# One layer of a two-block network on one core: S5 outputs one gate unit earlier, groups of seven, and a later second HGRN operand

## What is computed

```python
h = rms_norm(x, mix_norm[l])
(u_a, q_b, f_b, i_b, og_b, cx_c, v_c, o_c, ig_c, fg_c, gates) = jnp.split(h @ w_in[l], splits, axis=-1)
y_a = s5_mixer(u_a, ...)      # complex diagonal recurrence, 32 groups of 16, 64 states
y_b = hgrn2_mixer(q_b, f_b, i_b, og_b, ...)   # gated linear attention, 6 heads, chunks of 64
y_c = mlstm_mixer(cx_c, v_c, o_c, ig_c, fg_c, ...)
merged = (sigmoid(g_a) * (y_a @ wb[:r_a]) + sigmoid(g_b) * (y_b @ wb[r_a:r_b])
          + sigmoid(g_c) * (y_c @ wb[r_b:]))
x = x + merged @ w_out[l]
```

## Time and profile before

| what | value |
|---|---|
| median of 3 runs | 3008.32 us (3007.78 to 3015.89) |
| the profiled execution's own time | 3018.68 us |
| its span in the profile | 3016.9 us |
| TensorE busy (matmuls) | 2962.8 us, 98% of the span |
| VectorE busy | 2051.3 us, 68% |
| ScalarE busy | 1311.4 us, 43% |
| mean granted TensorE clock | 0.994 |
| DMA | 530.39 MB, 176 GB/s |

### The profile page before, as it was taken

One profiled execution on the slowest core, in us unless ns is written; L12 is line 12 of the kernel. 1 busy time (PEld: TensorE's weight loads), 2 busy tenths in 40 slices (PEclk: granted clock), 3 DMA queues, 4 the chain that ended last, 5 costly groups with the idle time before them and its releaser, 6 DMA issues.

```text
span 3016.9 us, 47095 instructions
## 1 busy us (share of the span) xinstructions
PE 2962.8 (98%) x18616; PEld 2640.7 (88%) x18616; DVE 2051.3 (68%) x2624; ACT 1311.4 (43%) x1418; POOL 70.3 (2%) x72
## 2 busy tenths in 40 slices
PE   8999999889999999999999999999999999999999
PEld 8898898889988888888888888886998888888888
DVE  6674787866778888885557776636667666666444
ACT  5354424334444444444444344425444444444333
POOL 0000000000001000000000000000000000000000
PEclk9999999999999999999999999999999999999999
DMA  6553334445555555555555554531455555555555
GB/s 227 182 188 131 119 112 141 140 134 202 183 193 195 195 193 191 190 184 184 187 188 200 194 182 167 182 136 56 168 181 195 191 190 191 194 194 179 193 194 186
DMA packets 87359, 530.39 MB, mean 176 GB/s; under 512 B 9952, under 2 KB 10336, under 8 KB 41184
## 3 DMA queue, kind: packets, MB, share of 16 engines
q1 hardware_dynamic: 87264, 529.07, 50.4%
HBM read 526.94 MB, written 2.10 MB: 175 GB/s over the span
## 4 chain that ended last, share of the span: by engine, by line
PE 94%; DVE 4%; ACT 1%; issue 0%; DMA 0%; SPq 0%; DVEq 0%; ACTq 0%
PE bank L576 72%; PE late L576 22%; DVE arena L1670 2%; DVE half_low L1670 1%; DVE arena L1667 0%; DVE w_low L1670 0%; ACT w_high L1186 0%; DVE arena L1972 0%; PE late L1127 0%; DMA xT<-in_xT 0%; DMA ring<-in_w_gates 0%; DVE acts_both L1670 0%; DVE arena L2087 0%; DVE arena L2088 0%; DVE arena L2030 0%
## 5 line engine op out<-in xcount | busy, mean ns | idle before, releaser
L1670 DVE TENSOR_TENSOR w_low<-ring,w_high 128x2048 fp32r<-128x2048 f32 (+1 forms) x480 | 1014.4, 2114 | 388.4 <-ACT w_high L1186 384.5
L1186 ACT ACTIVATE w_high<-ring 128x2048 fp32r<-128x2048 f32 (+1 forms) x480 | 849.5, 1771 | 649.4 <-DMA ring<-in_w_down 225.9
L576 PE MATMUL bank<-up_early,w_high 128*128 128x512 f32 x1408 | 487.8, 389 | 0.0
L576 PE MATMUL bank<-up_late,w_high 128*128 128x512 f32 x1408 | 487.4, 389 | 0.0
L576 PE MATMUL late<-acts_both,w_high 128*128 128x512 f32 x1408 | 485.8, 392 | 0.3 <-DVE w_low L1670 0.3
L576 PE MATMUL late<-acts_both,w_low 128*128 128x256 f32 x1408 | 391.7, 278 | 0.0
L576 PE MATMUL bank<-up_early,w_low 128*128 128x256 f32 x1408 | 388.7, 276 | 0.0
L576 PE MATMUL bank<-up_late,w_low 128*128 128x256 f32 x1408 | 388.6, 276 | 0.0
L576 PEld LDWEIGHTS late<-acts_both,w_high 128*128 128x128 f32 x1408 | 264.5, 188 | 58.4 <-DVE w_low L1670 0.6
L576 PEld LDWEIGHTS bank<-up_early,w_high 128*128 128x128 f32 x1408 | 264.3, 188 | 55.2
L576 PEld LDWEIGHTS bank<-up_late,w_high 128*128 128x128 f32 x1408 | 264.3, 188 | 55.1
(11 more groups left out here) (311 smaller groups left out, 5041.0 us busy)
## 6 DMA issues: line engine op xcount, KB each, us to landing
ring<-in_w_up SPq DMA_DIRECT2D x176, 1024.0 KB, 4.7
ring<-in_w_down SPq DMA_DIRECT2D x128, 704.0 KB, 4.0
ring<-in_w_in SPq DMA_DIRECT2D x66, 1024.0 KB, 4.7
ring<-in_w_mix SPq DMA_DIRECT2D x62, 1024.0 KB, 4.8
ring<-in_w_gates SPq DMA_DIRECT2D x96, 512.0 KB, 3.7
ring<-in_w_branch SPq DMA_DIRECT2D x16, 1024.0 KB, 4.8
ring<-in_w_out SPq DMA_DIRECT2D x16, 1024.0 KB, 4.7
ring<-in_w_o SPq DMA_DIRECT2D x16, 1024.0 KB, 4.7
```

The costliest lines, as they stand in the source:

```text
L576: return nc.tensor.matmul(o, lhsT, rhs, start=first, stop=last)
L1186: A(w_high[:, s, 0:cols], ring[:, s, 0:cols], ACT.Copy).then_inc(rounded[s], 1)
L1670: return V.tensor_tensor(o, a, b, op)
```

## The change

It does five things in the first block's mixing part. (1) TensorE issues each S5 output one gate unit earlier (after units 23, 30, 37 and 44; before it was after 24, 31, 38 and 43), and the feeds of tiles 2 and 3 after units 27 and 34 in place of 26 and 33. (2) VectorE's `s5_kept(f - 1)` moves from before the four products from PSUM to behind the two sums, where only a wait for the output stays before the products (they overwrite what that output's matmuls read). Each of the tiles 1 to 3 now has seven lowerings. Before these were six, seven and seven; tile 0 has five in place of four. One lowering stands in the middle of the scans. (3) The output matrix is made in two parts, the second behind the last rotation. (4) In the HGRN levels `meet(2)` and the lowering of gate unit 8 move behind the copies of level 0, and the memset of `HPR` moves to before the mLSTM's normalisation. (5) The first two branch units do their 12 HGRN and mLSTM k-tiles first, without the wait for `s5_gate`, and then their 4 S5 k-tiles. The number of instructions on SyncE, TensorE and ScalarE is the same, and SyncE's order is unchanged.

```diff
-GATES_FED = 44
+GATES_FED = 46
...
@@ TensorE
             for c in range(19, GATES_FED):
                 gate()
-                if c in (21, 26, 33):
-                    s5_feed({21: 1, 26: 2, 33: 3}[c])
-                if c in (24, 31, 38):
-                    s5_output({24: 0, 31: 1, 38: 2}[c])
-            s5_output(3)
+                if c in (21, 27, 34):
+                    s5_feed({21: 1, 27: 2, 34: 3}[c])
+                if c in (23, 30, 37, 44):
+                    s5_output({23: 0, 30: 1, 37: 2, 44: 3}[c])
             for c in range(GATES_FED, GATES):
                 gate()
...
-            def branches(first):
-                def body(s):
-                    for o, lo, hi in ((bank[s][:, 1], 4, 10), (bank[RING + s][:, 0], 10, 16), (bank[s][:, 0], 0, 4)):
-                        if first:
-                            pe.wait_ge(y_lowered, 3 if lo == 0 else 2)
-                            pe.wait_ge(s5_gate, 1)
-                        for k in range(lo, hi):
-                            last = mm3(o, s, k, *y[k], k == lo, k == hi - 1)
-                    return last
-                return body
...
+            def branch_parts(s, first):
+                for o, lo, hi in ((bank[s][:, 1], 4, 10), (bank[RING + s][:, 0], 10, 16)):
+                    if first and lo == 4:
+                        pe.wait_ge(y_lowered, 2)
+                    for k in range(lo, hi):
+                        mm3(o, s, k, *y[k], k == lo, k == hi - 1)
...
+            pair = []
+            for j in range(2):
+                s, _, _, _, free = units.next(split=True)
+                pe.wait_ge(lowered[s], units.lowered[s].value())
+                if not isinstance(free, int) or free > 0:
+                    pe.wait_ge(drained[s], free)
+                branch_parts(s, j == 0)
+                pair.append(s)
+            pe.wait_ge(y_lowered, 3)
+            for s in pair:
+                branch_s5(s).then_inc(consumed[s], 1)
+            for j in range(2):
+                unit_split(branches)
+            rounds_split(3, branches)
...
@@ VectorE, the way into the HGRN levels
             row_factors()
             lower_gate()
+            V.memset(HPR, 1.0)
             dve.wait_ge(norm_spread, casts[0])
...
             dve.wait_ge(norm_done, 2)
 
 
-            lower_gate()
-            link(V.memset(HPR, 1.0))
             dve.wait_ge(hg_x, 1)
-            dve.wait_ge(hmask_landed, 16)
             meet(1)
-            meet(2)
+            dve.wait_ge(hmask_landed, 16)
+
             for lvl in range(9):
                 dve.wait_ge(hg_scored, lvl + 1)
...
-                if 1 <= lvl <= 6:
+                if lvl == 0:
+                    lower_gate()
+                if lvl <= 6:
                     meet(lvl + 2)
                 if lvl < 8:
                     lower_gate()
...
@@ VectorE, S5
-            def s5_output_matrix():
+            def s5_output_matrix(part):
...
-                    s5_kept(f - 1)
+                    dve.wait_ge(s5_out, f)
                 dve.wait_ge(s5_fed, f + 1)
...
                 if f == 0:
-                    s5_output_matrix()
+                    s5_output_matrix(0)
+                else:
+                    s5_kept(f - 1)
                 lower_gate()
                 for n in range(4):
                     m = mag[:, 4 * f + n:4 * f + n + 1].broadcast_to([P, T])
                     V.tensor_tensor_scan(tmp_r[:, n], m, SR[:, n], 0.0, M, ADD)
                     last = V.tensor_tensor_scan(tmp_i[:, n], m, SI[:, n], 0.0, M, ADD)
+                    if n == 1:
+                        lower_gate()
                 link(last)
                 lower_gate()
                 link(tt(SR, turn_c, tmp_r))
                 link(tt(SI, turn_s, tmp_r))
                 link(tt(tmp_r, turn_s, tmp_i))
                 tt(tmp_i, turn_c, tmp_i).then_inc(s5_states, 1)
+                dve.wait_ge(s5_states, f + 1)
+                if f == 0:
+                    s5_output_matrix(1)
                 lower_gate()
-                dve.wait_ge(s5_states, f + 1)
-                if f > 1:
-                    lower_gate()
-            s5_kept(S5_TILES - 1)
             for c in range(GATES_FED, GATES):
                 lower_gate()
+                if c == GATES_FED + 1:
+                    s5_kept(S5_TILES - 1)
```

More of the change, by code:

```diff
@@ L972, in _, with branch_s5, branches @@
                 y += [(y_high[:, 6 * m + k], y_low[:, at + k]) for k in range(6)]
-            def branches(first):
-                def body(s):
-                    for o, lo, hi in ((bank[s][:, 1], 4, 10), (bank[RING + s][:, 0], 10, 16), (bank[s][:, 0], 0, 4)):
-                        if first:
-                            pe.wait_ge(y_lowered, 3 if lo == 0 else 2)
-                            pe.wait_ge(s5_gate, 1)
-                        for k in range(lo, hi):
-                            last = mm3(o, s, k, *y[k], k == lo, k == hi - 1)
-                    return last
-                return body
[L985 to L988, removed]
+            def branch_parts(s, first):
[4 more added lines that the diff above has]
+                        mm3(o, s, k, *y[k], k == lo, k == hi - 1)
+            def branch_s5(s):
+                for k in range(4):
+                    last = mm3(bank[s][:, 0], s, k, *y[k], k == 0, k == 3)
+                return last
+            def branches(s):
+                branch_parts(s, False)
+                return branch_s5(s)
+            pair = []
[12 more added lines that the diff above has]
+            rounds_split(3, branches)
             merged_out(out_both)
@@ L1979, in _ @@
             lower_gate()
[L1981 to L1986, removed]
-            lower_gate()
[L1988 to L1995, removed]
-            lower_gate()
-            link(V.memset(HPR, 1.0))
-            dve.wait_ge(hg_x, 1)
-            dve.wait_ge(hmask_landed, 16)
             def halves(ap, B):
@@ L2018, in meet @@
                     link(tt(pf[:, :, 1], pf[:, :, 1], pf[:, :, 0, B - 1:B].broadcast_to(n)))
+            for h in range(HG):
+                last = (V.tensor_scalar(HF[:, h], HF[:, h], lb[:, 1, h:h + 1], lb[:, 0, h:h + 1], M, ADD))
+            link(last)
+            V.tensor_scalar(HK, HF, -1.0, 1.0, M, ADD).then_inc(hg_x, 1)
+            V.memset(PD, 0.0)
+            row_factors()
+            lower_gate()
+            V.memset(HPR, 1.0)
+            dve.wait_ge(norm_spread, casts[0])
+            for h in range(ML):
+                for k, p0, p1, _ in PIECES[h]:
+                    c = VAT["ml_norm"] + k
+                    last = stt(HH[p0:p1, k], HH[p0:p1, k], vec[p0:p1, c:c + 1], factor(h)[p0:p1])
+            link(last)
+            tt(MT[:, O0:O0 + 6], HH, MT[:, O0:O0 + 6]).then_inc(norm_done, 1)
+            dve.wait_ge(norm_done, 2)
+            dve.wait_ge(hg_x, 1)
             meet(1)
-            meet(2)
+            dve.wait_ge(hmask_landed, 16)
             for lvl in range(9):
@@ L2048, in _ @@
             lower_gate()
-            def s5_output_matrix():
+            def s5_output_matrix(part):
                 re, im = (x.rearrange("p (n o) -> p n o", o=1).broadcast_to([P, S5_STATES, S5_ROWS]) for x in (cr, ci))
[L2052 to L2058, removed]
+                if part == 0:
+                    dve.wait_ge(s5_c_landed, 16)
+                    link(tt(c_new, c_re, re))
+                    link(tt(c_tmp, c_im, im))
+                    link(tt(c_new, c_new, c_tmp, SUB))
+                else:
+                    link(tt(c_tmp, c_re, im))
+                    link(tt(c_im, c_im, re))
+                    tt(c_im, c_im, c_tmp, ADD).then_inc(s5_c_made, 1)
             def s5_kept(f):
```

1 line of the change is left out of this document (removed).

## The result

The changed kernel takes 2984.13 us (median of 4 runs, 2982.29 to 2985.54), the kernel before 3012.11 us (median of 4, 3007.78 to 3017.72). The ratio is 0.9906, 95% interval 0.9884 to 0.9927: 28 us, 0.9%, less. Forecast were 27.2 us less and 2981.1 us. The profiled execution took 2985.54 us, 33.1 us less than that of before, which is more than the medians differ. Counted up to the 37th matmul of the branch units, close to where the change ends, the two traces differ by 26.8 us (696.03 against 669.26 us from the first matmul). Of these, 0.8 us lie ahead of 366 us, before the first instruction that the change moves; the profiles of this study differ by up to 1.2 us there. So 26.0 us are the change's: 0.7 in the HGRN stretch, 24.2 in the S5 stretch, 1.1 at the branch units. The rest of the 33.1 comes later and is not the change's.

What follows compares the result with a forecast made beforehand. The prediction took TensorE's waits and its matmuls' clock as the bound. Gains of 25.5 (S5), 0.5 (HGRN) and 1.2 us (branch units) sum to 27.2, from 3008.3 to 2981.1 us, range 2975 to 2994.

Steps and rivals of the forecast that it cites:

- What bounds: Whole kernel: TensorE carries 94% of the chain, so only its waits and the speed of its matmuls can move the time.
- S5 stretch, 25.5 us: 479 to 695 us: today's 21.1 us of waits and 6.5 of clock fall to about 2.1, gain 25.5 us.
- 5.85: Time in us taken for one undisturbed gate unit on TensorE, between 5.93 and 5.75 from the profile.
- the bound: S5 stretch: VectorE has about 4.4 us for other work between lowerings before the next unit's first half is late.
- `s5_kept` and the earlier output: S5 tiles 1 to 3: with output one unit earlier, VectorE finds it done; three waits of 0.2 us remain.
- VectorE's load, 42.5 of 45.4 us: S5 group of seven units: VectorE's work takes about 42.5 us, TensorE's units, output and feed 45.4.
- the rival that rests on its load: S5 groups of seven: VectorE stays slower, TensorE waits 4.1 us a group, 2993.4 us in all; chance 0.15.
- HGRN, 0.5 us: HGRN levels: cost 7.6 us becomes 7.1, with new waits of 1.3 and 4.1 and 1.7 for the clock.
- Branch units, 1.2 us: First branch units: waits of 1.75 and 0.69 us become one of 1.2 ahead of unit 1, gain 1.2 us.
- The loads did not become the bound: Rival on gate halves' loads: landings slow to 8.7 us, TensorE waits in each of 29 units, 3017 us; chance 0.03.
- nothing was given back: Rival on later stages: weights arrive no sooner, branch and output stages wait for them, about 3008 us; chance 0.05.
- HGRN did not get worse: Rival in HGRN levels: two new waits and low clock through unit 8 and level 1, loss 3.4 us; chance 0.07.
- The low end: Lower end of the forecast range, 2975 us: the forecast with all waits gone, 32.2 us gain.

## Why the prediction was right, point by point

- *What bounds.* Right. The gain came from waits (16.8 us in the S5 stretch) and from the clock (7.4 us less busy time for the same matmuls).
- *S5 stretch, 25.5 us.* Measured 24.2: from the first feed to the gated linear unit's end it took 222.7 us before and 198.5 after. Two sizes were off and partly cancelled, which is luck: waits gave 16.8 us where 19.0 were forecast, and the clock 7.4 where 6.5 were. (By the prediction's own rows the three units ran 2.6 + 2.6 + 1.6 = 6.9 us over 5.85; it rounded this down to 6.5. What it left of waits, 1.0 + 0.4 + 0.6, adds to 2.0, not 2.1.) The waits left came at each of the places forecast, and nowhere else. Ahead of unit 21 it is 0.99 us (1.0 forecast), ahead of output 0 0.67 (0.4). Ahead of units 27, 34 and 41 it is 0.48, 0.80 and 1.57, where I had 0.2 each. This is the mis-sized term: 2.85 us instead of 0.6. The chain of waits after, ahead of unit 41:

```profile
612.29 4.79 DMA ring<-in_w_gates
617.07 0.02 issue
617.10 1.07 ACT half_high L1385
...
620.46 3.48 DVE arena L1684 x3
623.95 0.02 issue
623.97 1.23 DVE half_low L1684
```

This half landed after 4.79 us. I took the landing at its median of 3.7 us as if it were fixed. The half lowered just ahead of the products landed after 3.70, 4.01 and 4.79 us at the three places, and each wait is the landing less 3.2 us: with a piece over the bound there is no slack, and TensorE waits for all that is late. In another trace of the same kernel the same halves took 3.74, 3.85 and 4.04 us, and the waits were 0.52, 0.64 and 0.83. Late landings are 1.4 of the 2.85 us. The other 0.85 over the forecast are mostly the bound itself: a unit between two others took 5.76 us by its starts, not the 5.85 that I used, so two units gave 0.2 us less cover, and at a landing of 3.7 us a wait is 0.5, not 0.2. In three traces of this kernel the total in the stretch is 3.4, 4.5 and 4.8 us.
- *`s5_kept` and the earlier output.* The prediction costed them together and gave no share to either. The runs show that VectorE's dealing of lowerings does it, and that TensorE's earlier output is a second way to the same end: 14.2 us alone, nothing on top.
- *VectorE's load, 42.5 of 45.4 us.* Right: between the products of tiles 2 and 3 (572.55 to 619.33 us) VectorE was busy 41.1 of 46.8 us, and the rival that rests on its load fell. VectorE waits 23.0 us for roundings in the stretch, 14 times, but it does so where it is ahead.
- *HGRN, 0.5 us.* Right in every part: waits of 1.38 and 3.94 us (1.3 and 4.1 forecast), half clock behind the second, level 1 without a wait, and 0.7 us gained, in the traces of before and after and again with the part undone. The rule of the Trainium skill (TensorE: Matmul & The Clock Gate, "What's actually happening"), that activity releases the throttle, gave the direction. The trace agrees: 0.55 granted from 382.2 to 385.4 us. But the wait of 2.3 us behind S5's last output, ahead of unit 44, was followed by full clock in one kernel and half clock in another, so a wait of that length has either price. For waits of 1.2 and 2.0 us too the traces show half clock behind them. The forecast took full clock behind its waits of 1.0 to 1.3 us, and got it in all three traces of the changed kernel.
- *Branch units, 1.2 us.* Measured 1.1 from the gated linear unit's last matmul to the branch units' 37th. Waits of 2.4 have become one of 1.55, where I had 1.2. Without the wait for `s5_gate` unit 0's first matmul starts 0.36 us before the gated linear unit's last one ends, so TensorE was at unit 1 sooner than I took it to be; unit 1's lowering ended 5.7 us behind that end, as assumed.
- *Rivals.* The loads did not become the bound, and nothing was given back behind 720 us that the change caused. HGRN did not get worse.
- *The number.* 27.2 us forecast, 26.0 by the traces' stretches, 28 by the medians. The forecast started from a median of 3008.3 us; over four runs that of before is 3012.1, so with the same gain 2984.9 was to be expected; it took 2984.1. The low end was said to be all waits gone, 32.2 us; but that leaves the HGRN waits of 5.4 us in, and 3008.3 - 32.2 is 2976, not 2975.

## What to carry to other kernels

Where two engines with hand-written orders hand work to each other, count the background units that lie between the producer's instruction and the consumer's wait, and what stands behind that wait: with none between, each engine waits for the other in turn, and the slot-fed engine's pause can cost a second time through its clock (here 7.4 us beside 16.8 us of waits). Put the lowering (whatever feeds the busiest engine) first behind each hand-over, and keep the pieces of other work between two of them shorter than the unit's time less the supply chain's, worked out with a late load and not a median one; a piece near that bound turns every late load into a wait. Follow a small gain past the place where it arises: one of 1.8 us here was gone by 900 us. Undo the parts of a change one by one: here the part that it is named after was worth nothing beside the other.

## What the runs showed of the hardware that I had not expected

**A slower pace at full clock.** The same matmuls ran 3% slower in some executions, at a granted clock of 1.00 and with no wait. The first down projection from 1382 to 1572 us, two executions of the changed kernel, the groups of both (busy us, mean ns of one | idle):

```profile
L576 PE MATMUL late<-acts_both,w_high 128*128 128x512 f32 x560 | 190.4, 389 | 0.0
```

```profile
L576 PE MATMUL late<-acts_both,w_high 128*128 128x512 f32 x544 | 190.4, 395 | 0.0
```

In the first a matmul of 512 columns and one of 256 start 226 and 114 ns apart, in the second 233 and 117, through the whole of this projection (7.0 us longer), and not in the second block's projection with the same code. Of the twelve profiles of this study six have the one spacing and six the other. The kernel before has the longer one, two of the three profiles of the changed kernel as well, the first shown the shorter one. The same two spacings show in the output projections. The first block's, near 800 us, had the longer one in two of the twelve (2.7 us), and these are just the two kernels that lower branch unit 1 first. The second block's had it in the profile of before alone (2.6 us). What decides it was not found.

**Half clock behind a wait of 1.2 us.** In the second block's mixing part, near 2030 us, TensorE waits 1.18 us at the same matmul in all twelve profiles. About 2 us behind it the granted clock fell to 0.50 for 6.8 us in six of them, the first of the changed kernel among them, and stayed at 1.00 in the other six, the kernel before among them. It cost 3.0 to 3.1 us each time. So one wait of the same length at the same matmul has either price here, and it does not go with a kernel: one profile of the changed kernel has it and two have not.

The 7.0 us and the 3.0 are most of the 8 to 12 us by which executions of one kernel differ. This is why gains of 1 to 6 us were read from the traces up to 710 us and not from the medians.
